# A two-layer transformer block on one Trainium2 core: latent attention's value product turned over, its probabilities divided first, and the order of work around the mixers changed

## The chip, the cores and the metric

The kernel runs on one core of a Trainium2 chip. The time is that of the device for one execution, in microseconds (us), median of several runs; lower is better. The engines are TensorE (PE in the rows; its weight loads are PEld), VectorE (DVE), ScalarE (ACT), GpSimd (POOL), and SyncE (SP), which issues most of the transfers.

## The reference

Two layers, each of three sublayers on 256 tokens of width 1024: a gated feed-forward (width 2816), a mixer, another feed-forward. Around each stands a modulation from the condition `c` and a layer norm of the scaled residual. The mixer of layer 0 is a hybrid of windowed attention and a gated recurrence; that of layer 1 is latent attention:

```python
def mla(h, pos, w_down, q_norm, kv_norm, w_uq, w_ukv, w_out):
    cq, ckv, kr = jnp.split(h @ w_down, [C_Q_RANK, C_Q_RANK + C_KV_RANK], axis=-1)
    q = (rms_norm(cq, q_norm) @ w_uq).reshape(bsz, seq, C_HEADS, C_NOPE + C_ROPE)
    kv = (rms_norm(ckv, kv_norm) @ w_ukv).reshape(bsz, seq, C_HEADS, C_NOPE + C_V)
    ...
        s = (jnp.einsum('bqhd,bkhd->bhqk', qn_i, k_nope)
             + jnp.einsum('bqhr,bkr->bhqk', qr_i, k_rope)).astype(F32) * scale
        p = jax.nn.softmax(s, axis=-1).astype(v.dtype)
        return jnp.einsum('bhqk,bkhd->bqhd', p, v)
    ...
    return o.swapaxes(0, 1).reshape(bsz, seq, C_HEADS * C_V) @ w_out
```

There are 16 heads with keys of 64+32 and values of 64. Everything is float32.

## The kernel before

Tokens lie in two tiles of 128 (t = 0, 1). A projection is three matmuls: each factor is split into a high part and the rest (`w_hi`/`w_lo` for weights, `hT_hi`/`hT_lo` for the transposed activations), and hi*hi, lo*hi and hi*lo are added in PSUM (`product`, L1910, L1913, L1914). Weights come in slots of up to 128x2048 through three raw buffers; ScalarE rounds a slot into `w_hi` (`split_hi`), VectorE subtracts to get `w_lo` (`split_lo`, L1231), and a matmul on a slot waits on `lo_ready` of it. The six sublayers run one after another: feed-forward, hybrid, feed-forward, feed-forward, latent attention (MLA), feed-forward. Between sublayers a seam normalizes the residual, transposes it on TensorE (`enter`, `enter_second`) and makes `hT_hi`/`hT_lo` on ScalarE and VectorE.

Latent attention works in 16 units m of two heads and one token tile (`mla_unit`), heads in four groups g of four. The order on every engine comes from a list written out by hand, `mla_plan`; VectorE has its own, `mla_vector_plan`. Round n holds S of unit n (scores, two 96-deep matmuls of 256 columns, L2032; VectorE takes the negated maximum, L1734; ScalarE takes the exponential and its sum, L1104), P of unit n-1 (four transposes of the probabilities, L2043; VectorE copies them out as `mpT`, L1740, and takes the reciprocal of the sum, L1744) and V of unit n-2 (values, four matmuls with the probabilities stationary, 64 columns each, L2055; ScalarE scales by the reciprocal into `m_o`, L1113). The tables `before` and `behind` put the pieces of the projections uq and ukv, the transposes of queries and keys (`qkT`, L2022), the splits of weights and the pieces `out` of the output projection around the rounds. `owin` transposes `m_o` (four times four transposes, L2068), ScalarE and VectorE take its high and low part (L1122, L1753), and `out` multiplies with it. V uses one PSUM bank, bank 5, so V of a unit waits until the unit before it is out of that bank: in this kernel on `o_att`, which ScalarE raises behind L1113.

The hybrid mixer has one list for all engines, `hybrid_plan`. In a feed-forward, `take_lo` (L1790) makes the low part of the gated activations, and ScalarE's first `silu` (L1007) needs another activation table than what a mixer leaves loaded.

Of the kernel before, what the change touches and what calls it, by code (L numbers as in the profile page):

```python
# [13 lines left out]
F32 = mybir.dt.float32  # L14
# [29 lines left out]
def build(nc, A, out):  # L44
# [11 lines left out]
    with ExitStack() as ctx:  # L56
# [34 lines left out]
        neg_half = sb("neg_half", [P, 1])  # L91

# [173 lines left out]
        rden_ready = sem("rden_ready")  # L266
        freq_ready = sem("freq_ready")
# [120 lines left out]
        def hybrid_plan():  # L388

            yield from (("proj", 0), ("proj", 1), ("enter", 1), ("split", 3), ("lb", 0), ("proj", 2),  # L390
                        ("piece", 56), ("piece", 57), ("split", 4), ("scale", 0), ("split", 5), ("lb", 1), ("proj", 3), ("split", 6), ("kT", 0),
# [24 lines left out]

        OWIN = (0, 3)
# [9 lines left out]
        def mla_plan():  # L427
# [6 lines left out]
            before = {1: (("rq", (1, 1)),), 3: (("qkT", (1, 0)),), 4: (("uq", (2, 0)), ("rq", (2, 0))),  # L434
                      5: (("uq", (2, 1)), ("rq", (2, 1))), 6: (("ukv", (2, 0)),), 7: (("qkT", (2, 0)), ("ukv", (2, 1))),
                      8: (("uq", (3, 0)), ("rq", (3, 0)), ("uq", (3, 1))), 9: (("rq", (3, 1)), ("ukv", (3, 0)), ("ukv", (3, 1))),
                      12: (("out", (0, 0, 0)),), 13: (("out", (0, 0, 1)),), 14: (("out", (1, 0, 0)),), 15: (("out", (1, 0, 1)),),
                      16: (("out", (2, 0, 0)),)}
            behind = {1: (("hi", (7, 0, 1)),), 2: (("hi", (8, 0, 1)),), 3: (("qkT", (1, 1)),), 4: (("hi", (9, 0, 1)),),
# [13 lines left out]
            yield from (("out", (3, 0)), ("split", (16, 0, 1)), ("owin", (1, 1)), ("end", 0), ("out", (0, 1)), ("out", (1, 1)),  # L453
                        ("out", (2, 1)), ("next", 0), ("out", (3, 1)))

        def mla_vector_plan():
# [5 lines left out]
            inner = {1: (("rq", (1, 1)),), 11: (("owin", (0, 0)),), 12: (("owin", (1, 0)),), 15: (("owin", (0, 1)),)}  # L462
# [6 lines left out]
            for n in range(18):  # L469
                if n < 16:  # L470
                    yield "S", n
                yield from inner.get(n, ())
                if n == 9:
                    yield "qkT", (3, 0)
                if 0 < n < 17:
                    yield "P", n - 1
# [1987 lines left out]
```

## Time and profile before

| | |
|---|---|
| median of 3 runs | 1029.35 us (1028.67 to 1029.74) |
| profiled execution | 1028.7 us, its span 1026.7 us |
| TensorE busy | 1000.4 us, 97% of the span |
| VectorE / ScalarE busy | 807.3 us (79%) / 501.8 us (49%) |
| MLA, 725 to 850 us from the span's start | TensorE 122.38 of 125 us busy, VectorE 102.66, ScalarE 81.89 |

A row of a timeline gives start, duration, engine, line, operation, operands and count; in brackets stands the engine's idle time before it and what ended that. The ends of matmuls are modelled and overlap their successors, so the pace of TensorE is read from starts, not from durations.

### The profile page before, as it was taken

The page shows a single profiled execution, that of the slowest core. Times are in us where ns is not written, and L with a number is a line of the kernel's source. Part 1 is how long each engine was busy: PE and PEld are TensorE (multiplying, and loading weights), DVE is VectorE, ACT ScalarE, POOL GpSimd, SP SyncE. Part 2 cuts the span into 40 slices and gives each one's busy share as a digit, 9 for nine tenths or more (in the row PEclk, how much of TensorE's full clock was granted, in tenths as well). Part 3 has the DMA queues.
Part 4 walks back from the last instruction along what each step waited for, and adds up shares of the span by engine and source line. Part 5 has one row for each costly group of instructions (what it writes and reads, how often), then busy time and mean ns, then how long its engine had stood idle before and what let it go on. Part 6 is the DMA issues. An engine that isn't in the chain of part 4 may idle for free.

```text
span 1026.7 us, 13208 instructions
## 1 busy us (share of the span) xinstructions
PE 1000.4 (97%) x5024; PEld 830.1 (81%) x5024; DVE 807.3 (79%) x1203; ACT 501.8 (49%) x754; POOL 47.6 (5%) x101
## 2 busy tenths in 40 slices
PE   7999999999999999999999999999999999999996
PEld 5678888879978788888887888888888878888885
DVE  5989898678989897888778878877788886666455
ACT  4654344366767544343545343443677554444430
POOL 1000000011311000000000000000100000000000
PEclk9999999999999999999999999999999999999999
DMA  9999998458423699979848997974323559656431
GB/s 352 409 363 409 385 373 317 161 185 278 154 108 120 207 379 343 318 276 340 296 149 317 337 325 274 386 252 136 93 98 101 165 180 332 230 203 242 168 123 41
DMA packets 72545, 254.80 MB, mean 248 GB/s; under 512 B 8801, under 2 KB 10337, under 8 KB 72482
## 3 DMA queue, kind: packets, MB, share of 16 engines
q1 hardware_dynamic: 68946, 242.91, 65.5%
q0 software_dynamic: 3104, 10.39, 3.1%
q8 instruction: 40, 0.66, 0.2%
q10 hardware_dynamic: 432, 0.66, 0.2%
q14 instruction: 23, 0.19, 0.1%
HBM read 252.85 MB, written 1.07 MB: 247 GB/s over the span
## 4 chain that ended last, share of the span: by engine, by line
PE 82%; DVE 7%; ACT 4%; DMA 4%; issue 2%; DVEq 0%; SPq 0%; ACTq 0%
PE bank L1910 25%; PE bank L1914 24%; PE bank L1913 24%; DMA w_raw<-in_w_dram 3%; PE bank L2321 2%; DVE w_lo L1231 2%; DMA arena<-in_ada_w_dram 1%; PE bank L2032 1%; PE bank L2055 1%; PE bank L2022 1%; ACT w_hi L885 1%; PE bank L2043 1%; ACT arena L919 1%; ACT hT_hi L913 0%; PE bank L1883 0%
## 5 line engine op out<-in xcount | busy, mean ns | idle before, releaser
L1231 DVE TENSOR_TENSOR w_lo<-w_raw,w_hi 128x2048 fp32r<-128x2048 f32 (+3 forms) x162 | 345.1, 2149 | 25.5 <-ACT w_hi L885 25.5
L1910 PE MATMUL bank<-w_hi,hT_hi 128*128 128x512 f32 (+3 forms) x880 | 351.2, 399 | 8.9 <-DVE hT_lo L1769 4.2
L1914 PE MATMUL bank<-w_lo,hT_hi 128*128 128x512 f32 (+3 forms) x880 | 338.9, 385 | 0.0
L1913 PE MATMUL bank<-w_hi,hT_lo 128*128 128x512 f32 (+3 forms) x880 | 338.3, 384 | 0.0
L885 ACT ACTIVATE w_hi<-w_raw 128x2048 fp32r<-128x2048 f32 (+3 forms) x152 | 281.1, 1852 | 37.3 <-DMA w_raw<-in_w_dram 27.1
L1910 PEld LDWEIGHTS bank<-w_hi,hT_hi 128*128 128x128 f32 x880 | 165.9, 189 | 44.9 <-DVE hT_lo L1769 5.9
L1914 PEld LDWEIGHTS bank<-w_lo,hT_hi 128*128 128x128 f32 x880 | 165.7, 188 | 33.5
L1913 PEld LDWEIGHTS bank<-w_hi,hT_lo 128*128 128x128 f32 x880 | 166.4, 189 | 28.7
L1007 ACT ACTIVATE arena<-bank 128x256 f32<-128x256 f32 x88 | 33.6, 382 | 279.8 <-PE bank L1914 279.7
L1250 DVE SCALAR_TENSOR_TENSOR arena<-arena,c_row 128x1024 f32<-128x1024 f32 x131 | 155.8, 1219 | 8.0 <-ACT c_row L960 7.7
L1910 PE MATMUL bank<-w_hi,fT_hi 128*128 128x512 f32 x352 | 138.4, 393 | 1.1 <-DVE fT_lo L1790 0.7
L1914 PE MATMUL bank<-w_lo,fT_hi 128*128 128x512 f32 x352 | 137.4, 390 | 0.0
L1913 PE MATMUL bank<-w_hi,fT_lo 128*128 128x512 f32 x352 | 137.1, 389 | 0.0
L1785 DVE TENSOR_TENSOR arena<-arena,bank 128x256 f32<-128x256 f32 x88 | 36.9, 419 | 77.7 <-ACT arena L1007 77.6
L1790 DVE TENSOR_TENSOR fT_lo<-bank,fT_hi 128x256 fp32r<-128x256 f32 x88 | 37.2, 423 | 57.6 <-ACT fT_hi L1011 57.6
L1910 PEld LDWEIGHTS bank<-w_hi,fT_hi 128*128 128x128 f32 x352 | 66.1, 188 | 16.2 <-issue 1.7
L1914 PEld LDWEIGHTS bank<-w_lo,fT_hi 128*128 128x128 f32 x352 | 66.1, 188 | 13.9
L1913 PEld LDWEIGHTS bank<-w_hi,fT_lo 128*128 128x128 f32 x352 | 66.1, 188 | 13.2
L1011 ACT ACTIVATE fT_hi<-bank 128x256 fp32r<-128x256 f32 x88 | 33.7, 383 | 78.3 <-PE bank L2321 78.3
L1910 PE MATMUL bank<-hT_hi,w_hi 128*128 128x256 f32 x128 | 36.6, 286 | 0.5 <-DVE w_lo L1231 0.5
L1914 PE MATMUL bank<-hT_lo,w_hi 128*128 128x256 f32 x128 | 36.2, 283 | 0.0
L1913 PE MATMUL bank<-hT_hi,w_lo 128*128 128x256 f32 x128 | 36.2, 283 | 0.0
(242 smaller groups left out, 863.3 us busy)
## 6 DMA issues: line engine op xcount, KB each, us to landing
w_raw<-in_w_dram SPq DMA_DIRECT2D x306, 512.0 KB, 5.6
arena<-in_ada_w_dram SPq DMA_DIRECT2D x132, 512.0 KB, 7.3
m_o<-in_ada_w_dram SPq DMA_DIRECT2D x10, 512.0 KB, 6.9
gate_row<-gate_scratch POOLq DMA_DIRECT2D x6, 512.0 KB, 5.0
arena<-in_ln_g_dram POOLq DMA_DIRECT2D x6, 512.0 KB, 4.8
arena<-in_ln_b_dram POOLq DMA_DIRECT2D x6, 512.0 KB, 6.1
w_raw<-in_w_dram SPq DMA_DIRECT2D x8, 256.0 KB, 2.8
w_raw<-in_w_dram SPq DMA_DIRECT2D x8, 192.0 KB, 2.8
```

What stands on the lines that cost most here:

```text
L885: nc.scalar.activation(w_hi[:, j0 % RING, 0:n], raw_of(j0)[:, 0:n], ACT.Copy).then_inc(hi_ready, 1)
L919: op = nc.scalar.activation(scratch[:, k * P:(k + 1) * P], second_block(s, k), ACT.Identity, bias=mod_B[:, s, k:k + 1], scale=mod_G[:, s, ...
L1007: nc.scalar.activation(sg[:, i % 2, :], unit_bank(s, i)[:, 0:CW], ACT.Silu).then_inc(silu_done, 1)
L1011: nc.scalar.activation(fT_hi[:, i % 2, :], T[i % 2][:, 0:CW], ACT.Copy).then_inc(fT_hi_ready, 1)
L1231: op = nc.vector.tensor_tensor(w_lo[:, j0 % RING, c], raw_of(j0)[:, c], w_hi[:, j0 % RING, c].bitcast(F32), ALU.subtract)
L1250: nc.vector.scalar_tensor_tensor(out=raw, in0=raw, scalar=1.0, in1=c_row[:, :], op0=ALU.mult, op1=ALU.mult, accum_out=mod_col[:, a:a + 1]) ...
L1785: nc.vector.tensor_tensor(hid[:, i % 2, :], sg[:, i % 2, :], unit_bank(s, i)[:, CW:2 * CW], ALU.mult)\
L1790: nc.vector.tensor_tensor(fT_lo[:, i % 2, :], T[i % 2][:, 0:CW], fT_hi[:, i % 2, :].bitcast(F32), ALU.subtract).then_inc(fT_ready, 1)
L1910: mm = nc.tensor.matmul(dst, a_hi, b_hi, start=start, stop=False)
L1913: nc.tensor.matmul(dst, a_lo, b_hi, start=False, stop=False)
L1914: return nc.tensor.matmul(dst, a_hi, b_lo, start=False, stop=stop)
L2321: mm = nc.tensor.transpose(T[i % 2][:, q * P:(q + 1) * P], hid[:, i % 2, q * P:(q + 1) * P], ident[:, :])
```

## The change

In MLA: V's operands change places, so that the values (128x64 of a head) are stationary and the transposed probabilities move (128 columns); the two heads of a unit write partitions 0 to 63 and 64 to 127 of bank 5, and the output is transposed already. ScalarE copies it to `hT_hi` (new stage V there) and VectorE subtracts for `hT_lo` (`values_lo`, L1766 of the new kernel); V of a unit now waits on `o_ready`, which VectorE raises behind that subtraction. `m_o`, the `owin` stages and their evictions go. The probabilities are divided before they are transposed: stage D on VectorE takes the reciprocal and multiplies the two heads' probabilities in place, and P waits on `p_ready`. The copy of the transposed probabilities moves from VectorE to ScalarE. The latent activations move to k = 4 to 7 of `hT_hi`/`hT_lo`. The output bank of token tile 1 is 6 and 7, so that `out` pieces of it can stand inside the rounds, and the tables are written anew.

Elsewhere: ScalarE runs a one-element Silu before the entry of the feed-forward behind a mixer; VectorE splits slot 2 of a feed-forward before `take_lo` of its first unit; in the hybrid, ScalarE enters the second token tile before it evicts projection 1, and splits and pieces change places.

```diff
+        def mla_block(m):
+            g, t, p = mla_unit(m)
+            return 2 * g + p, slice(t * P, (t + 1) * P)
+        M_UNITS = {(0, 0): 2, (0, 1): 4, (1, 0): 6, (1, 1): 8, (2, 0): 10, (3, 0): 12, (2, 1): 14, (3, 1): 16}
...
+            before = {4: (("uq", (2, 0)),), 5: (("uq", (2, 1)),), 6: (("ukv", (2, 0)),), 3: (("qkT", (1, 0)),),
+                      7: (("qkT", (2, 0)), ("ukv", (2, 1))), 8: (("uq", (3, 0)), ("uq", (3, 1))),
+                      9: (("ukv", (3, 0)), ("ukv", (3, 1))), 10: (("out", (0, 0)),), 11: (("out", (0, 1)),),
+                      12: (("out", (1, 0, 0)),), 13: (("out", (1, 0, 1)),), 14: (("out", (2, 0)),), 15: (("out", (3, 0)),),
+                      16: (("out", (1, 1)),), 17: (("out", (2, 1)),)}
...
+            for n in range(16):
+                yield from early.get(n, ())
+                yield "S", n
+                if n >= 3:
+                    yield "V", n - 3
                 yield from inner.get(n, ())
+                yield "D", n
                 yield from outer.get(n, ())
-            yield from (("split", (16, 0, 1)), ("owin", (1, 1)), ("end", 0))
+            yield from (("end", 0), ("V", 15), ("lo", (16, 1)), ("scale", (1, 1)))
...
# ScalarE
+                        elif stage == "P":
+                            act.wait_ge(p_tr, A0 + m + 1)
...
+                            nc.scalar.activation(mpT[:, m % 2, :], banks[4][:, :], ACT.Copy).then_inc(pT_ready, 1)
                         elif stage == "V":
+                            k, tok = mla_block(m)
                             act.wait_ge(pv_done, A0 + m + 1)
...
+                            nc.scalar.activation(hT_hi[:, k, tok], banks[5][:, 0:P], ACT.Copy).then_inc(o_hi, 1)
...
+                    if early_third(s - 1):
+                        nc.scalar.activation(early_silu[:, :], neg_half[:, :], ACT.Silu)
...
# VectorE
-                        norm(s, 0)
+                        values_lo(13)
+                        norm(s, 0, lambda: (values_lo(14), split_lo(base[s] + 16, (0,))))
...
-                        nc.vector.tensor_copy(mpT[:, m % 2, :], banks[4][:, :]).then_inc(pT_ready, 1)
+                    elif stage == "D":
+                        b = m % 2
                         dve.wait_ge(s_exp, A0 + m + 1)
...
+                        step(nc.vector.reciprocal(rden[:, m % 4, :], den[:, m % 4, :]))
+                        step.wait()
+                        for a in range(2):
+                            op = nc.vector.tensor_scalar(mP[:, b, a, :], mP[:, b, a, :], rden[:, m % 4, a:a + 1], None, ALU.mult)
+                        op.then_inc(p_ready, 1)
...
+            def values_lo(m):
+                k, tok = mla_block(m)
+                dve.wait_ge(o_hi, O0 + m + 1)
+                nc.vector.tensor_tensor(hT_lo[:, k, tok], banks[5][:, 0:P], hT_hi[:, k, tok].bitcast(F32),
+                                        ALU.subtract).then_inc(o_ready, 1)
...
+                        if i == 0:
+                            split_lo(base[s] + 2)
                         take_lo(i)
...
# TensorE
-                        pe.wait_ge(s_exp, A0 + m + 1)
+                        pe.wait_ge(p_ready, m + 1)
...
-                            pe.wait_ge(o_att, A0 + m)
-                        for a in range(2):
-                            h = 2 * p + a
-                            for kt in range(NT):
-                                c = (2 * a + kt) * P
-                                mm = nc.tensor.matmul(banks[5][:, a * 64:a * 64 + 64], mpT[:, m % 2, c:c + P],
-                                                      v_nat[g][:, kt, h * 64:h * 64 + 64],
-                                                      start=kt == 0, stop=kt == 1)
+                            pe.wait_ge(o_ready, O0 + m)
+                        for kt in range(NT):
+                            for a in range(2):
+                                h, c = 2 * p + a, (2 * a + kt) * P
+                                mm = nc.tensor.matmul(banks[5][a * 64:a * 64 + 64, 0:P], v_nat[g][:, kt, h * 64:h * 64 + 64],
+                                                      mpT[:, m % 2, c:c + P], start=kt == 0, stop=kt == 1,
+                                                      skip_group_check=True)
                         mm.then_inc(pv_done, 1)
-                    elif stage == "owin":
...
-                        for k in range(4):
-                            c = (4 * half + k) * P
-                            mm = nc.tensor.transpose(banks[6 + t][:, k * P:(k + 1) * P], m_o[:, t, c:c + P], ident[:, :])
```

VectorE's queue in rounds 12 and 13 of MLA, before; each row is an instruction and the semaphores it waits on (`COPY` is the eviction of the transposed probabilities, `w_lo` the split of half a slot, `x<-x,arena` the scaling by the norm's rows):

```order
L1734 TENSOR_REDUCE neg_max<-bank2 128x2 [waits s_exp,s_done]
L1753 TENSOR_TENSOR hT_lo<-bank7,hT_hi 128x4x128 [waits o_hi]
L1740 COPY spare_row<-bank4 128x512 [waits pv_done,p_tr]
L1744 RECIPROCAL rden<-den 128x2 [waits o_att,s_exp]
L1231 TENSOR_TENSOR w_lo<-w_raw,w_hi 128x1024 [waits hi_ready]
L1672 TENSOR_TENSOR x<-x,arena 128x1024 [waits dve_step]
L1734 TENSOR_REDUCE neg_max<-bank3 128x2 [waits s_exp,s_done]
L1740 COPY spare_row<-bank4 128x512 [waits pv_done,p_tr]
L1744 RECIPROCAL rden<-den 128x2 [waits o_att,s_exp]
L1231 TENSOR_TENSOR w_lo<-w_raw,w_hi 128x1024 [waits hi_ready]
```

VectorE's queue in round 14 and up to D of round 15, after (`hT_lo<-bank5` is `values_lo`; the first `w_lo` of the `x2` row is the second half of the slot of `out` (3, 0)):

```order
L1749 TENSOR_REDUCE neg_max<-bank2 128x2 [waits s_exp,s_done]
L1766 TENSOR_TENSOR hT_lo<-bank5,hT_hi 128x128 [waits o_hi]
L1244 TENSOR_TENSOR w_lo<-w_raw,w_hi 128x1024 [waits hi_ready]
L1754 RECIPROCAL rden<-den 128x2 [waits s_exp]
L1757 TENSOR_SCALAR arena<-arena,rden 128x256 [waits dve_step]
L1757 TENSOR_SCALAR arena<-arena,rden 128x256
L1244 TENSOR_TENSOR w_lo<-w_raw,w_hi 128x1024 [waits hi_ready] x2
L1749 TENSOR_REDUCE neg_max<-bank3 128x2 [waits s_exp,s_done]
L1766 TENSOR_TENSOR hT_lo<-bank5,hT_hi 128x128 [waits o_hi]
L1244 TENSOR_TENSOR w_lo<-w_raw,w_hi 128x1024 [waits hi_ready]
```

The subtraction that frees bank 5 stands behind the maximum of the same round, and the multiplications of D stand between the two halves of a slot.

TensorE's queue in round 14 and at the beginning of round 15, after (bank 2 and 3 hold scores, bank 4 the transposed probabilities, bank 5 the values' product; `lo_ready4` is the slot of `out` (3, 0)):

```order
L2053 MATMUL bank2<-arena 128x256 [waits s_exp,qk4_ready]
L2053 MATMUL bank2<-arena 128x256
L2064 MATMUL bank4<-ident,arena 128x128 [waits pT_ready,p_ready]
L2064 MATMUL bank4<-ident,arena 128x128 x3
L2075 MATMUL bank5<-spare_row,arena 64x128 [waits o_ready,pT_ready]
L2075 MATMUL bank5<-spare_row,arena 64x128 x3
L1930 MATMUL bank0<-w_hi,hT_hi 128x512 [waits lo_ready4,o_ready]
```

In the kernel before, the row of V reads as this, in the same place between P and the next piece:

```order
L2043 MATMUL bank4<-ident,arena 128x128 [waits pT_ready,s_exp]
L2043 MATMUL bank4<-ident,arena 128x128 x3
L2055 MATMUL bank5<-arena,spare_row 128x64 [waits o_att,pT_ready]
L2055 MATMUL bank5<-arena,spare_row 128x64 x3
```

V's wait changed from ScalarE's semaphore to VectorE's, P's from the exponential to the division, and an output piece stands where a projection stood.

## Rows read from the trace of the kernel before

**Rows 1.** The page: busy time, and the chain that ended last by engine

```profile
PE 1000.4 (97%) x5024; PEld 830.1 (81%) x5024; DVE 807.3 (79%) x1203; ACT 501.8 (49%) x754; POOL 47.6 (5%) x101
PE 82%; DVE 7%; ACT 4%; DMA 4%; issue 2%; DVEq 0%; SPq 0%; ACTq 0%
```

**Rows 2.** Busy time by stage: PE, PEld, DVE, ACT, POOL, PEclk, DMA share, GB/s

```profile
725.00:850.00 125.00, 122.38 (x738) 106.08 (x738) 102.66 (x202) 81.89 (x210) 5.13 (x8) 1.00 0.40 134
```

**Rows 3.** Timeline of one round of MLA: start, us, engine, instruction

```profile
774.04 1.03 PE L2032 MATMUL bank<-arena 96*128 96x256 f32 x4
...
774.91 0.60 PE L2043 MATMUL bank<-ident,arena 128*128 128x128 f32 x4
775.11 0.69 DVE L1734 TENSOR_REDUCE neg_max<-bank 128x2 f32<-128x512 f32 x1 [0.73 <-PE bank L2032]
775.35 1.00 PE L2055 MATMUL bank<-arena,spare_row 128*128 128x64 f32 x8
775.72 0.68 DVE L1740 COPY spare_row<-bank 128x512 f32<-128x512 f32 x1
775.83 0.47 ACT L1104 ACTIVATE arena<-bank,neg_max 128x256 f32<-128x256 f32 x1 [0.75 <-DVE neg_max L1734]
776.19 1.04 PE L2022 MATMUL bank<-ident,arena 128*96 128x128 f32 x8
...
776.75 0.51 ACT L1113 ACTIVATE m_o<-bank,rden 128x64 f32<-128x64 f32 x2
```

**Rows 4.** Chain of waits, in the hybrid: scores of two heads

```profile
307.51 0.63 PE bank L2185 x4
```

**Rows 5.** Groups by line and shape: count, busy us, mean ns, idle before

```profile
L1278 DVE TENSOR_TENSOR hT_lo<-arena,hT_hi 128x128 fp32r<-128x128 f32 x10 | 2.5, 288 | 1.9 <-ACT hT_hi L913 1.5
...
L1744 DVE RECIPROCAL rden<-den 128x2 f32<-128x2 f32 x16 | 2.5, 155 | 0.0
...
L1562 DVE TENSOR_SCALAR arena<-arena 128x64 f32<-128x64 f32 x16 | 3.6, 270 | 0.0
...
L1469 DVE TENSOR_SCALAR x<-x,mean_var,rstd 128x1024 f32<-128x1024 f32 x5 | 4.1, 814 | 3.4 <-POOL rstd L779 3.4
...
L1231 DVE TENSOR_TENSOR w_lo<-w_raw,w_hi 128x1024 fp32r<-128x1024 f32 x14 | 16.9, 1210 | 1.3 <-ACT w_hi L885 1.3
...
L1395 DVE TENSOR_TENSOR arena<-bank,gate_row 128x512 f32<-128x512 f32 x12 | 7.7, 685 | 4.3 <-PE bank L1914 4.3
...
L1192 ACT ACTIVATE win_pT<-bank 128x512 f32<-128x512 f32 x8 | 4.7, 588 | 0.0
```

**Rows 6.** Timeline of TensorE: first P, and scores of unit 4

```profile
755.03 0.66 PE L2043 MATMUL bank<-ident,arena 128*128 128x128 f32 x4
...
762.80 1.03 PE L2032 MATMUL bank<-arena 96*128 96x256 f32 x4
```

**Rows 7.** Timeline of TensorE: half an output piece, a wait, the next entry

```profile
809.53 0.50 PE L1910 MATMUL bank<-w_hi,hT_hi 128*128 128x512 f32 x1
...
811.05 0.60 PE L2043 MATMUL bank<-ident,arena 128*128 128x128 f32 x4
...
789.32 1.13 PE L2032 MATMUL bank<-arena 96*128 96x256 f32 x4 [0.78 <-DVE arena L1725]
...
826.07 1.03 PE L1883 MATMUL bank<-ident,x 128*128 128x128 f32 x8
```

**Rows 8.** Timeline around the seams: a table load, and TensorE's waits

```profile
837.12 1.28 ACT L1007 ACT_TABLE_LOAD   x1
...
840.46 0.50 PE L1910 MATMUL bank<-w_hi,hT_hi 128*128 128x512 f32 x1 [0.69 <-DVE hT_lo L1285]
...
358.30 0.50 PE L1910 MATMUL bank<-w_hi,hT_hi 128*128 128x512 f32 x1 [0.71 <-DVE hT_lo L1285]
...
549.65 0.47 PE L1910 MATMUL bank<-w_hi,fT_hi 128*128 128x512 f32 x1 [0.47 <-DVE w_lo L1231]
...
218.87 0.63 PE L1896 MATMUL bank<-ident,x 128*128 128x128 f32 x4 [1.08 <-issue]
```

More of the change, by code:

```diff
@@ L388, in hybrid_plan @@
         def hybrid_plan():
-            yield from (("proj", 0), ("proj", 1), ("enter", 1), ("split", 3), ("lb", 0), ("proj", 2),
-                        ("piece", 56), ("piece", 57), ("split", 4), ("scale", 0), ("split", 5), ("lb", 1), ("proj", 3), ("split", 6), ("kT", 0),
+            yield from (("proj", 0), ("proj", 1), ("enter", 1), ("lb_pre", 0), ("split", 3), ("split", 4), ("lb", 0), ("proj", 2), ("hi", 5),
+                        ("piece", 56), ("lo", 5), ("piece", 57), ("scale", 0), ("lb", 1), ("proj", 3), ("split", 6), ("scale", 1), ("kT", 0),
                         ("proj", 4), ("split", 7), ("proj", 5), ("piece", 58), ("split", 8), ("proj", 6),
@@ L415, in hybrid_plan, with hybrid_scalar_plan @@
                         ("out", (3, 1)))
+        def hybrid_scalar_plan():
+            yield from (("proj", 0), ("enter", 0), ("enter", 1), ("proj", 1))
+            plan = hybrid_plan()
+            for stage, m in plan:
+                if (stage, m) == ("enter", 1):
+                    break
+            yield from plan
         OWIN = (0, 3)
@@ L452, in mla_plan @@
                 yield from behind.get(n, ())
-            yield from (("out", (3, 0)), ("split", (16, 0, 1)), ("owin", (1, 1)), ("end", 0), ("out", (0, 1)), ("out", (1, 1)),
-                        ("out", (2, 1)), ("next", 0), ("out", (3, 1)))
+            yield from (("next", 0), ("out", (3, 1)))
         def mla_vector_plan():
@@ L548, in out_banks @@
         def out_banks(s, t):
-            return ([banks[0], banks[5]], [banks[6], banks[7]])[t] if subs[s][0] == "hyb" else Y[t]
+            if subs[s][0] == "ffn":
+                return Y[t]
+            return ([banks[0], banks[5 if subs[s][0] == "hyb" else 1]], [banks[6], banks[7]])[t]
         def entry_banks(s):
@@ L718, in _ @@
                         if kind == "hyb":
[L719 removed]
+                            for a in {7: (58,), 8: (59,), 12: (60,), 13: (61,), 14: (62, 63)}.get(j - base[s], ()):
                                 ada_piece(a)
@@ L1496, in hybrid @@
                     elif stage == "scale":
-                        scale_shift(s, 0)
-                        scale_shift(s, 1)
+                        scale_shift(s, m)
                     elif stage in ("split", "lo"):
                         split_lo(base[s] + m)
-                    elif stage == "lb" and m == 0:
+                    elif stage == "lb_pre":
                         logits = cols[:, 96:108].rearrange("p (v h) -> p v h", v=3)
@@ L1509, in hybrid @@
                         op.then_inc(lb_pre, 1)
-                    elif stage == "lb":
+                    elif stage == "lb" and m == 1:
                         dve.wait_ge(lb_exp, 1)
@@ L1832, in _ @@
                             split_lo(base[s] + n)
-                        if i == 0 and not early_third(s):
-                            split_lo(base[s] + 2)
                         for n in end_slots(i):
@@ L1999, in mla @@
                             w, tok = slice(k * width, (k + 1) * width), slice(t * P, (t + 1) * P)
-                            mm = product(bank[:, 0:width], hT_hi[:, 2 * v + k, tok], hT_lo[:, 2 * v + k, tok],
+                            at = M_LATENT + 2 * v + k
+                            mm = product(bank[:, 0:width], hT_hi[:, at, tok], hT_lo[:, at, tok],
                                          w_hi[:, j0 % RING, w], w_lo[:, j0 % RING, w], k == 0, k == 1)
@@ L2078, in hybrid @@
+                        out_project(s, i, t, MOUT, range(4), {i: O0 + M_UNITS[i, t]}, q or (0, 1))
             def hybrid(s):
```

87 lines of the change are left out of this document (26 added, 61 removed), and 13 rows, old and new, of tables (behind, inner, outer).

## The prediction

> **What bounds the kernel now.** I read the page first: TensorE is busy 97% of the span and holds 82% of the chain that ended last, VectorE 7%, ScalarE and the transfers 4% each [rows 1]. So time goes when TensorE's stream gets shorter, and comes when TensorE waits. Then the table of stages: from 725 to 850 us, around latent attention (MLA), TensorE is busy 122.38 of 125 us at a granted clock of 1.00 (the 2.4 GHz level), VectorE 102.66 [rows 2]. Its waits there are few; the largest in the rounds is 0.78 us [rows 7]. Then one round in time [rows 3]: S starts at 774.04, P at 774.91, V at 775.35, the next work at 776.19. TensorE's pace is thus 0.87 for S, 0.44 for P, 0.84 for V, with nothing between. VectorE begins the maximum 0.20 behind the start of P, and its next instruction comes 0.61 later. I call the end of S (start of P) T in what follows.
>
> **The change part by part, TensorE's own work.** V has 4 matmuls, recorded as 8 passes, 0.105 us each, though they move only 64 columns. After, they move 128. A pass of 256 columns takes 0.87/4 = 0.217 [rows 3], so one of 128 takes 0.108. If the two heads' column halves work side by side, a pass of one head lies over a pass of the other. No instruction of the trace uses column halves. The nearest is the hybrid's scores, two heads in row halves, four passes of 256 columns: 0.63 us, three passes' time, not four [rows 4]. By that pattern 8 passes take the time of 5: 0.54 us, 0.30 less than before. The other bound is no overlap, 8 x 0.108 = 0.86, 0.02 more. I take the pattern of rows 4: 16 x 0.30 = -4.8. The four groups of transposes of `m_o` go, each like a P: 4 x 0.44 = -1.8. The 0.78 wait before a score [rows 7] goes with the copy that left VectorE's queue. TensorE in MLA: -7.4.
>
> Against the pattern stands a rule of the Trainium skill (TensorE: Matmul & The Clock Gate, Part 3, The mechanism): a weight load overlaps a matmul in flight only when the two are in different row groups. Column halves share their rows. By that rule each pass would show its load as well; if a load of 64 columns takes half of V's present pace, 0.053, V would take 8 x (0.108 + 0.053) = 1.29 us, 0.45 more than before, and the sum would be 12.0 higher, 1050. The trace does not bear it out: V's passes follow each other at 0.105 us with full-height loads between them [rows 3], so such loads are already hidden. I give it 2%.
>
> **What V waits for.** This decides the result. V of a unit needs bank 5 free of the unit before. Before, ScalarE freed it a round earlier. Now VectorE does, and its queue has, in round n, the maximum of unit n, then `values_lo` of unit n-3; TensorE has, in round n, S of n, P of n-1, V of n-2, which needs exactly that `values_lo`. So V cannot start before T + 0.20 + 0.61 (maximum, rows 3) + 0.29 (a 128x128 subtraction, rows 5) + about 0.05 for the semaphore = T + 1.15. P ends at T + 0.44. TensorE stands for 0.71 us; queued behind V are the projections, the output pieces and the next S, on which VectorE and ScalarE wait in turn. Rounds 4 to 8 and 10 to 15 have it: 11 x 0.71 = +7.8. In round 9 a transpose stage lies between and covers it, but the second one then waits about 0.5 for its bank: +0.5.
>
> D: reciprocal 0.16 [rows 5], a step's wait, two multiplications of 256. Rows 5 give 0.27 for 64 columns and 0.81 for 1024 as bounds; by the line between them 256 take about 0.38, the second overlapping a little. D takes some 0.9. The exponentials end near T + 1.95 (776.75 plus the last readout, rows 3), so P of the next round is free at T + 2.9 to 3.2. From round 3 on, T' is at least 3.7 later, so D costs TensorE nothing there.
>
> At the start it does. VectorE now waits for the first exponential (ready by 755.03, where P starts, rows 6) and divides before it takes the second maximum. P of unit 0 starts 1.0 later. The second exponential starts near 756.6, and behind it ScalarE has the eviction of a ukv piece and the new copy of the probabilities (0.59, rows 5): P of unit 1 finds its bank copied only at about 759.1, with TensorE idle for 1.9. Then V of unit 1 waits for `values_lo` behind a half split, D and a pair of copies: about 1.6. Unit 4's scores start near 766.7 instead of 762.80 [rows 6]. That is +3.9 with two V savings inside, +4.5 of waits.
>
> **Output pieces.** A half split takes 1.21 [rows 5]. `out` (1, 0) and (2, 0) stand right behind V, at T + 1.69, but their slot's second half is split behind `values_lo`, done at T + 2.3: 0.65 each, +1.3. `out` (3, 0) is worse: its second half stands behind D, ends near T + 4.4, and TensorE is there at T + 1.69: +2.7.
>
> **The end of MLA.** An output piece takes two times 1.52 less overlap, about 2.8 [rows 7]. With T the end of the last S: P, V of 13, `out` (1, 1), P of 15 end at T + 5.0; V of 14 needs `values_lo(13)`, which now stands behind D (T + 3.1) and the four 512-wide instructions of the residual (0.6 to 0.69 each, rows 5), T + 5.9: +0.9. The next entry's transposes (826.07 in the kernel before, rows 7) come without a wait. But behind them VectorE has `values_lo(15)`, a half split and a scaling of 1.2 each before it enters the feed-forward, which puts TensorE's first product there 0.8 late, and the second tile's entry about 1.2 more. Tail: +2.9.
>
> MLA in sum: -7.4 + 7.8 + 0.5 + 4.5 + 1.3 + 2.7 + 2.9 = +12.3.
>
> **Seams and hybrid.** The early Silu takes the 1.28 table load [rows 8] out of the path to the second entry; ScalarE was idle before it. That ends the waits of 0.69 and 0.71 [rows 8]. The third split before `take_lo` ends one of 0.47 [rows 8]. In the hybrid, ScalarE stood behind projection 1 while TensorE waited 1.08 for the entry [rows 8]; now it enters first. Half of this can return at the weight splits that come next. I take 1.0. Sum: -2.9. ScalarE has room for the copies it takes on (49% busy, rows 1).
>
> Total +9.4 on the profiled 1028.7, or on the median 1029.35: 1038.7. Estimates of small waits tend to add what overlaps, so I round down to 1038.
>
> The Trainium skill (TensorEngine Tiling (Array Packing), Key Properties) says that a change of tiling mode drains TensorE, and V would change it twice a unit, 32 times. It gives no figure; rows 4 show three full passes in 0.63 us between full-height work, so nothing of a drain is visible for row halves. At the 0.16 us between a 1.03 us modelled duration and the 0.87 pace [rows 3], 32 would make +5.1, and the sum 1043.
>
> **The rivals.**
> 1. No overlap of the halves, or a drain at each switch (12%): then V costs 0.02 more, not 0.30 less; +5.1, 1043. For it: no row has column halves. Against it: rows 4. Nothing hides it, since V is on the path in every round.
> 2. Faster (19%): V's wait doesn't bind. This holds if `values_lo` is done when P ends, that is when VectorE needs under T + 0.44 for what stands before it; it decides from there, since each tenth more costs 1.1 us over 11 rounds. Then -7.4 - 2.9 = -10.3 remain, less waits at the start that are there anyway: about 1019 to 1023. Against it: the maximum cannot start before S ends and takes 0.61 alone.
> 3. It cancels (6%): V's wait is real (+8.3), but the weight splits, the start and the end cost about 2 instead of 11.4, since the engines behind catch up: near 1029.
> 4. The gain is not made at all in V because VectorE becomes the bound: its round is then 0.61 + 0.29 + 1.21 + 0.9 + 1.2 = 4.2, against 4.1 on TensorE in round 11. That is a part of the forecast's upper end, not a case of its own.
>
> **How the numbers follow.** Forecast 61%, 1033 to 1042 around 1038; rival 1 12%, rival 2 19%, rival 3 6%, loads in the open 2%. What a measurement can tell from no change is 0.2%, 2.1 us. Slower than 1031.4: 0.75; within: 0.05; faster than 1027.3: 0.20. The range of 8 in 10 takes in rivals 1 and 3 and the edge of 2: 1026 to 1044.
>
> **What would show it.** In the profile after: V's row 64x128 at 0.54 us pace (0.86 shows rival 1); in nearly each round a wait of TensorE of about 0.7 before V, released by VectorE's `hT_lo` (none shows rival 2); a wait of about 2.7 on `w_lo` before the first matmul of `out` (3, 0); P of unit 1 some 2.5 us later than before against S of unit 0; no table load between the entries; the waits at the three seams gone. The prediction is wrong if VectorE's `values_lo` is done before P ends, or if the rounds close up elsewhere.

## The result, and the profile after

The changed kernel takes 1039.53 us (median of 4 runs, 1038.78 to 1040.37) against 1029.01 of the kernel before beside it: ratio 1.0102, 95% interval [1.0084, 1.0119]. The profiled span grew from 1026.7 to 1037.0 us. In the page, against [rows 1]:

```profile
PE 997.6 (96%) x5008; PEld 823.2 (79%) x5008; DVE 807.7 (78%) x1233; ACT 504.4 (49%) x752; POOL 51.3 (5%) x101
PE 84%; DVE 7%; DMA 4%; ACT 3%; issue 2%; SPq 0%; DVEq 0%; ACTq 0%
```

TensorE is busy for 2.8 us less and stands idle for 13 us more. The table of stages shows where (columns as [rows 2]):

```profile
725.00:750.00 25.00, 24.35 (x156) 21.62 (x156) 18.46 (x53) 17.06 (x48) 2.69 (x4) 1.00 0.36 111
750.00:775.00 25.00, 19.70 (x137) 15.74 (x137) 19.37 (x53) 18.31 (x51) 0.00 (x0) 1.00 0.29 97
775.00:800.00 25.00, 21.42 (x136) 17.48 (x135) 16.55 (x40) 14.32 (x37) 0.00 (x0) 1.00 0.27 93
800.00:825.00 25.00, 19.18 (x104) 14.87 (x104) 16.19 (x29) 13.51 (x31) 0.00 (x0) 0.93 0.35 114
825.00:850.00 25.00, 22.99 (x123) 17.36 (x123) 20.70 (x44) 12.69 (x30) 2.45 (x4) 1.00 0.38 121
sum 125.00, PE 107.64 PEld 87.08 DVE 91.26 ACT 75.88 POOL 5.14; mean PE 21.53 PEld 17.42 DVE 18.25 ACT 15.18 POOL 1.03
```

Where 122.38 of 125 us were busy, 107.64 are, though no engine is full: VectorE fell from 102.66 to 91.26. In one stage the granted clock is 0.93, not 1.00. TensorE's waits over the whole kernel, by what ended them (total, times, longest):

```profile
PE bank L2075 <- DVE hT_lo L1766: 8.4, 13, 1.0
...
PE bank L1930 <- DVE w_lo L1244: 3.3, 3, 2.3
...
PE bank L1930 <- DVE fT_lo L1810: 2.3, 2, 1.9
...
PE bank L2064 <- ACT spare_row L1134: 1.4, 1, 1.4
PE bank L2053 <- DVE arena L1740: 1.2, 1, 1.2
PE bank L2064 <- DVE arena L1757: 1.0, 1, 1.0
```

L2075 is V, waiting for `values_lo`; L1930 with `w_lo` is an output piece waiting for the split of its slot; L2064 is P at the start. The wait on `fT_lo` is in the feed-forward layers, not in latent attention. One round of the new kernel in time, to be read beside [rows 3]:

```profile
771.06 1.03 PE L2053 MATMUL bank<-arena 96*128 96x256 f32 x4
...
771.92 0.60 PE L2064 MATMUL bank<-ident,arena 128*128 128x128 f32 x4
772.12 0.69 DVE L1749 TENSOR_REDUCE neg_max<-bank 128x2 f32<-128x512 f32 x1 [0.74 <-PE bank L2053]
772.73 0.28 DVE L1766 TENSOR_TENSOR hT_lo<-bank,hT_hi 128x128 fp32r<-128x128 f32 x1
...
773.16 0.66 PE L2075 MATMUL bank<-spare_row,arena 128*64 128x128 f32 x8 [0.63 <-DVE hT_lo L1766]
...
773.75 1.08 PE L2043 MATMUL bank<-ident,arena 128*96 128x128 f32 x8
```

S starts at 771.06, P 0.86 later, the maximum 0.20 behind P, `values_lo` 0.61 behind the maximum, and V 1.24 behind P, with 0.63 idle. V's pace is 773.75 - 773.16 = 0.59, where it was 0.84 (0.81 in front of a projection). The idle times are counted from modelled ends; by starts a V that need not wait stands 0.53 behind P (best2 below), so the wait moved it by 0.70. The fourth output piece shows the largest wait, and something that was not forecast:

```profile
818.80 0.31 PE L2075 MATMUL bank<-spare_row,arena 128*64 128x128 f32 x2
821.44 0.51 PE L1930 MATMUL bank<-w_hi,hT_hi 128*128 128x512 f32 x1 [2.33 <-DVE w_lo L1244]
821.75 0.63 PE L1933 MATMUL bank<-w_hi,hT_lo 128*128 128x512 f32 x1
822.18 0.63 PE L1934 MATMUL bank<-w_lo,hT_hi 128*128 128x512 f32 x1
822.60 0.63 PE L1930 MATMUL bank<-w_hi,hT_hi 128*128 128x512 f32 x1
```

and the stages there; the granted clock is the third number from the end of each row:

```profile
821.00:822.00 1.00, 0.56 (x2) 0.55 (x3) 1.00 (x2) 1.00 (x1) 0.00 (x0) 0.86 0.00 0
822.00:824.00 2.00, 2.00 (x6) 1.51 (x6) 0.43 (x1) 0.56 (x1) 0.00 (x0) 0.50 0.76 174
824.00:825.00 1.00, 1.00 (x4) 0.81 (x3) 0.00 (x0) 0.00 (x0) 0.00 (x0) 0.50 0.98 385
```

TensorE had worked 0.66 us in the 3.6 before 821.44. Then the granted clock fell from 1.00 to 0.50 (2.4 to 1.2 GHz), matmuls came every 0.43 us instead of 0.23, and the piece took 821.44 to 825.85, 4.41 us, where the third took 2.83.

### The profile page after: what moved, and what is told of

Its sections match the earlier page's. It is cut to its first block, busy times and chain, and to the rows that moved or that the text cites. A ratio compares the mean times of both kernels' runs of the same rounds, so it can differ in the third digit from the quotient of the medians.

```text
span 1037.0 us, 13173 instructions
## 1 busy us (share of the span) xinstructions
PE 997.6 (96%) x5008; PEld 823.2 (79%) x5008; DVE 807.7 (78%) x1233; ACT 504.4 (49%) x752; POOL 51.3 (5%) x101
## 4 chain that ended last, share of the span: by engine, by line
PE 84%; DVE 7%; DMA 4%; ACT 3%; issue 2%; SPq 0%; DVEq 0%; ACTq 0%
PE bank L1930 26%; PE bank L1934 26%; PE bank L1933 26%; DMA w_raw<-in_w_dram 3%; PE bank L2330 2%; DMA arena<-in_ada_w_dram 1%; DVE w_lo L1244 1%; PE bank L2053 1%; DVE neg_max L1749 1%; PE bank L2152 1%; PE bank L2075 1%; PE bank L2182 0%; PE bank L2043 0%; DVE x L1431 0%; ACT arena L939 0%
## 5 line engine op out<-in xcount | busy, mean ns | idle before, releaser
L1930 PE MATMUL bank<-w_hi,hT_hi 128*128 128x512 f32 (+3 forms) x880 | 351.5, 399 | 12.0 <-DVE hT_lo L1789 4.9
L1930 PEld LDWEIGHTS bank<-w_hi,hT_hi 128*128 128x128 f32 x880 | 166.4, 189 | 49.6 <-DVE hT_lo L1789 6.2
L1930 PE MATMUL bank<-w_hi,fT_hi 128*128 128x512 f32 x352 | 138.2, 393 | 2.3 <-DVE fT_lo L1810 2.3
L1930 PEld LDWEIGHTS bank<-w_hi,fT_hi 128*128 128x128 f32 x352 | 66.1, 188 | 16.2 <-DVE fT_lo L1810 2.9
L1930 PE MATMUL bank<-hT_hi,w_hi 128*128 128x256 f32 x128 | 36.5, 285 | 0.0
```

Of the source, the lines that this page charges most:

```text
L1930: mm = nc.tensor.matmul(dst, a_hi, b_hi, start=start, stop=False)
```

## The experiments

Milestones on TensorE make the traces comparable: when S of unit 0 starts, how long it is from there to the first transpose of the next layer's entry (latent attention), and from there to the start of the last matmul. All times in us:

| kernel | median | S of unit 0 | latent attention | after it |
|---|---|---|---|---|
| before | 1028.7 | 751.60 | 74.47 | 191.7 |
| changed | 1039.5 | 748.74 | 87.83 | 191.5 |
| seams_hybrid | 1023.6 | 748.06 | 74.47 | 190.1 |
| hybrid_alone | 1026.3 | 748.98 | 74.45 | 192.5 |
| seams_alone | 1026.1 | 751.77 | 74.46 | 190.1 |
| latent_alone | 1043.3 | 751.93 | 87.83 | 192.8 |
| heads_in_turn | 1038.8 | 748.00 | 87.80 | 191.6 |
| vlo_first | 1033.5 | 747.78 | 82.96 | 191.5 |
| slot14_early | 1036.2 | 748.79 | 84.35 | 191.5 |
| two_maxima | 1037.4 | 747.41 | 86.66 | 191.5 |
| best1 | 1026.1 | 748.35 | 76.08 | 191.0 |
| best2 | 1023.1 | 747.80 | 73.27 | 191.0 |
| best2b | 1025.4 | 748.06 | 75.28 | 190.9 |
| best3 | 1023.8 | 748.35 | 74.28 | 190.2 |

The median of the kernel before is the one beside the experiments (1028.53 to 1028.74 there). The third column varies by 1.4 among kernels that have the same instructions up to there as the changed one (747.41 to 748.79), so the fourth is the one that tells edits in latent attention apart.

**vlo_first.** Is V's wait a matter of VectorE's order?

```diff
-                yield "S", n
                 if n >= 3:
                     yield "V", n - 3
+                yield "S", n
```

> The changed kernel with one line of VectorE's order moved: in each round of latent attention values_lo of the unit three back stands ahead of the maximum, not behind it. TensorE's instructions are unchanged. Theory (V waits for values_lo only because it is queued behind the maximum): the 13 waits of 0.63 us in front of V (8.4 us by the waits view) go, or nearly, and what comes instead is at most the maximum 0.28 us later, which the exponential and then P may pass on in a few rounds: 1032 us against 1039.5 now (1030 to 1034). Rival 1 (VectorE or the chain of maximum, exponential, division is the bound of the round, so the wait only moves): the waits turn up in front of P or S with the same sum, 1038 to 1040. Rival 2 (the four V matmuls in alternate column halves cost the time, not the wait): no change, 1039.5.

1033.51 us, 6.0 less than the changed kernel, of which 4.9 lie in latent attention (the other 1.0 ahead of it, where the instructions are the same). TensorE's waits there:

```profile
PE bank L1930 <- DVE w_lo L1244: 4.8, 3, 2.9
...
PE bank L2053 <- DVE arena L1740: 2.2, 2, 1.9
...
PE bank L2075 <- DVE hT_lo L1766: 1.3, 2, 0.9
```

V's wait went from 8.4 to 1.3. Some of it came back (slots +1.5, a key and query copy +1.0), since TensorE now reaches the splits sooner. The theory holds; rivals 1 and 2 do not.

**slot14_early.** Did the clock fall because of the wait?

In short form (`inner` stands between maximum and division of a unit, `outer` behind the division):

```diff
-  inner 14: (("lo", (14, 0)),)     outer 13: (("scale", (1, 0)),)   outer 14: (("lo", (14, 1)),)
+  inner 14: (("lo", (14, 1)),)     outer 13: (("lo", (14, 0)),)     outer 14: (("scale", (1, 0)),)
```

> The changed kernel with the two halves of the split of weight slot 14 one step earlier on VectorE (in units 13 and 14), the scaling of x behind them. Theory: the wait of 2.33 us in front of the fourth output piece (821.44) goes, and with it the fall of TensorE's granted clock behind it, which made that piece 4.4 us long where the second and third piece took 2.8: 1039.5 - 2.3 - 1.6 = 1035.6 us. Rival 1 (the clock falls for what TensorE did before, not for the wait): the wait goes and the fall stays, 1037.2. Rival 2 (VectorE is the bound there, and the wait only moves to the third piece or the last V): 1039 to 1040.

1036.16 us, -3.4; latent attention 3.48 shorter. In the profiled execution (1035.39 us) the wait is 0.48 and the clock stays:

```profile
818.00:821.00 3.00, 2.04 (x14) 1.64 (x15) 2.96 (x7) 2.82 (x8) 0.00 (x0) 1.00 0.13 33
821.00:824.00 3.00, 2.93 (x16) 2.23 (x14) 1.94 (x3) 1.60 (x1) 0.00 (x0) 1.00 0.91 307
```

2.33 - 0.48 = 1.85 of wait and 4.41 - 2.83 = 1.58 of clock make the 3.4 between the two profiled executions. In vlo_first, whose slot wait is 2.89, the clock fell at the same place (0.50 from 817 to 820); in best3, whose longest wait in latent attention is 1.92, it did not. But this is one execution of each kernel. The fall in the changed kernel's trace lasted 3.4 us, which lowers the mean clock of an execution by about 0.0016, and the mean clock of the other executions of slot14_early is 0.997, 0.995, 0.996 and 0.996, against 0.998 in the profiled one (0.997 or 0.998 in every execution of best1, best2 and best3). The three at 0.995 and 0.996 are also its slowest, 1036.2 to 1037.4 us. So the clock very likely fell in them too, at a place that no trace shows: the edit took the fall away in the execution that was profiled, not in all.

**heads_in_turn.** Do the column halves run beside each other because the matmuls alternate between them?

```diff
-                        for kt in range(NT):
-                            for a in range(2):
+                        for a in range(2):
+                            for kt in range(NT):
```

> The changed kernel with V's four matmuls in another order: both of head a=0 (columns 0 to 63), then both of a=1, where now they alternate between the halves. Theory (the change's 0.59 us from start to next start, against 0.84 before, comes from alternating halves that run beside each other): V takes 0.75 to 0.85 us, 16 units at +0.16 to +0.26 are +2.5 to +4 us, less what the wait for values_lo takes back where V's end sets nothing: 1041.5 to 1043.5. Rival (four passes in 64 columns cost what they cost, and the order of halves is nothing): 1039.5.

1038.82 us; latent attention 87.80 against 87.83. V in the trace:

```profile
764.39 0.67 PE L2075 MATMUL bank<-spare_row,arena 128*64 128x128 f32 x8 [0.63 <-DVE hT_lo L1766]
764.99 0.45 PE L1930 MATMUL bank<-w_hi,hT_hi 128*128 128x384 f32 x1
```

Pace 0.60, as before the edit. My theory falls: the order of halves is nothing here. That they do overlap is shown all the same, since eight passes of 128 columns one behind another would take 0.86. The records of a V in either kernel have the starts of passes in pairs: 0.00, 0.01, 0.13, 0.17, 0.24, 0.28, 0.35, 0.39 us (changed kernel, V at 778.15), the next instruction at 0.59. Two by two at 0.109 a pair, and 0.20 from the last pass to the next work. How the hardware pairs them when the program issues one half first is open.

**seams_hybrid, hybrid_alone, seams_alone.** What do the side edits give? The first is the kernel before with both, the others with one each (in short form):

```diff
 (hybrid)  order of ScalarE: ("proj", 0), ("enter", 0), ("enter", 1), ("proj", 1); splits and pieces as in the change
 (seams)   + nc.scalar.activation(early_silu[:, :], neg_half[:, :], ACT.Silu)   ahead of the entry behind a mixer
 (seams)   + if i == 0: split_lo(base[s] + 2)   ahead of take_lo(0)
```

> The kernel before with only the side edits of the change: the hybrid layer's new order and the edits at the seams; latent attention is as before. Prediction on record for this part: -2.9 us, so 1026.1. By the trace of the changed kernel, first product of latent attention against before: -2.85 us, so 1026.2, if nothing is given back later. Rival (latent attention's start gives it back, since its weights then come too late or its first entry waits): 1028 to 1029.5, and then the latent part of the change costs only 10.5 us instead of 13.4.

> The kernel before with only the hybrid layer's new order, no seam edits. By the offsets between the traces, the hybrid layer gave 2.4 us up to its end (my price was 1.0): 1028.7 - 2.4 = 1026.3 us. Rival (the hybrid order only brings TensorE earlier to transfers and the seam gives it back, and the seam edits are what makes it stay): 1028 or more.

> The kernel before with only the seam edits of the feed-forward layers (the table of SiLU loaded early, the split of weight slot 2 ahead of take_lo). Both parts together measured -5.1 us. If the parts add up: -5.1 + 2.4 = -2.7, so 1026.0 us. My price on record was 0.69 + 0.71 + 0.47 = -1.9, so 1026.8. Rival (the table load is hidden without the hybrid order as well as with it, nothing gained): 1028.7.

1023.57 us together (ratio 0.9955 [0.9941, 0.9968]), 1026.32 and 1026.06 alone: -5.2, -2.2 and -2.5 against the before beside each. The hybrid's part shows by S of unit 0 (751.60 to 748.98): the wait of 1.08 [rows 8] is gone, and so are two that were in no sum, 0.53 for a split at 231.33 and 0.48 at 282.37 (0.07 is left of it). The seams' part shows only in the last layer (191.7 to 190.1), where the wait of 0.69 [rows 8] is gone (0.96 is gained at that place, the rest over the layer; that column varies by 0.8 between before and hybrid_alone, which have the same instructions there). Behind the hybrid the waits of 0.71 and 0.47 [rows 8] are gone too, but in seams_alone one of 1.05 for `fT_lo` stands in their place (at 371.11), and S of unit 0 comes at 751.77, no earlier than before. Expectation for the sum was 1026.1: missed by 2.5.

**latent_alone.** The change without the side edits.

> The change without its side edits: latent attention new, the hybrid layer's order and the seams as before. If the two halves of the change add up: the side edits gave -5.1 on the kernel before, the whole change is +10.5, so latent attention alone is +15.6: 1028.6 + 15.6 = 1044.2 us. By the traces' offsets (side edits gave only 2.85 us by the start of latent attention, and the last feed-forward layer in the changed kernel keeps 0.9 us of waits for its second entry, which the side edits alone do not have): 1028.6 + 13.4 = 1042 us. Rival on record (latent attention without overlap of the column halves costs more, and hides behind the seams' gain): 1046 or more.

1043.32 us, ratio 1.0148 [1.0134, 1.0162]: +14.6, between the two sums. So the side edits give 3.8 in the changed kernel and 5.2 in the kernel before, by the medians; by the traces' milestones it is 4.5 and 5.1 (3.2 and 1.3 against 3.5 and 1.6), so most of the difference is within what the traces vary. One source of that is seen: after the hybrid's seam TensorE waits for `take_lo`, which waits for ScalarE, which waits for a transfer of weights (6.03 us in the changed kernel). Depending on when the transfer landed, TensorE's wait was 1.86 us in the changed kernel (at 368.15), 1.0 in heads_in_turn and 0.5 in vlo_first, with the same instructions.

**two_maxima.** The start of latent attention: maximum 1 ahead of division 0.

```diff
                 yield "S", n
+                if n == 0:
+                    continue
+                if n == 1:
+                    yield "D", 0
```

> The changed kernel with one edit at latent attention's start on VectorE: the maximum of unit 1 stands ahead of the division of unit 0, not behind it. Theory (at the start P of unit 1 waits 1.44 us for ScalarE's copy, which stands behind the exponential of unit 1, which waits 1.5 us for its maximum, which is queued behind the division that waits for unit 0's exponential): the exponential of unit 1 starts 1.4 us earlier and P of unit 1 with it, 1039.5 - 1.4 = 1038.1 us. Rival (TensorE's next instructions wait for the division of unit 1 and for values_lo anyway, so the wait moves by a few rows): 1039.5.

1037.44 us (-2.1); latent attention 1.17 shorter. P of unit 1 no longer waits:

```profile
751.69 0.65 PE L2068 MATMUL bank<-ident,arena 128*128 128x128 f32 x4 [1.00 <-DVE arena L1761]
753.21 0.66 PE L2068 MATMUL bank<-ident,arena 128*128 128x128 f32 x4
```

Of the 1.44, 0.25 came back in V of unit 1 (a wait of 1.21 there, 0.96 in the changed kernel). The theory holds; the rest of the 2.1 lies ahead of the edit, inside the variation of the third column.

**best1, best2, best2b, best3.** Is the loss VectorE's order alone? TensorE's instructions are those of the change in all four.

```diff
 best1:  + "V", n-3 ahead of "S", n;  "S", 1 ahead of "D", 0;  qkT (2,1) ahead of lo (11,0);  scalings of x behind the splits
         + outer 10: lo (12,1)   outer 11: lo (13,0)   inner 12: lo (13,1)   inner 13: lo (14,0)   outer 13: lo (14,1)
         + values_lo(13) ahead of residual(s)
 best2b: + "V", n-2 behind "D", n instead;  inner 12: lo (13,0)   outer 12: lo (13,1)
 best2:  + best2b, and ScalarE's hi (14,1) behind unit 12
 best3:  + best2, qkT (1,0), (1,1) ahead of lo 7, lo 8;  the scalings of x one place earlier each
```

> The changed kernel with VectorE's order in latent attention made for the new waits: values_lo of three units back ahead of the maximum; maximum 1 ahead of division 0; the key and query copies (2,1) ahead of the split of slot 11; the halves of the splits of slots 12, 13 and 14 one step earlier and the scalings of x behind them; values_lo(13) ahead of the residual. TensorE's instructions are unchanged. Theory (waits on VectorE's order are the whole loss, the four V matmuls themselves are cheaper than before): 1039.5 - 6.0 (values_lo first, measured) - 3.4 (slot 14, measured) - 1.4 (start) - 1.9 (copies (2,1)) - 1.4 (slots 12 to 14, 0.48 each) - 0.9 (values_lo(13)) = 1024.5 us, so 1024 to 1028, about the kernel before with the side edits alone (1023.6). Rival (VectorE and the chain maximum, exponential, division fill the round, so waits come back in other places): 1030 or more.

> As best1, with values_lo two units back directly behind the division instead of three units back ahead of the maximum; the halves of the split of slot 13 behind maximum and division of unit 12; and on ScalarE the second half of the split of slot 14 one unit earlier. Theory (the waits left in best1's latent attention, 0.62 + 1.07 + 0.77 in front of V and 0.57 in front of P, come from VectorE instructions queued in front that wait for ScalarE's split, not from VectorE's amount of work): 1026.1 - 3.0 = 1023.1 us, so 1022.5 to 1024.5, level with or ahead of the kernel before with the side edits alone (1023.6). Rival (VectorE is full there and the waits come back elsewhere): 1025.5 to 1027.

> best2 without ScalarE's edit: the split of slot 14's second half stays behind unit 13. Theory: both halves of VectorE's split of slot 14 wait for ScalarE's second half, so the division of unit 13, which is queued behind the first, is late by about 1.5 us, of which 0.6 to 1.4 reaches TensorE: 1023.7 to 1024.5, about 1 us above best2. Rival (the slack in front of P of unit 13, a whole output piece, hides it): as best2.

> best2 with the last waits that its trace shows in latent attention taken up, on VectorE alone: the key and query copies (1,0) and (1,1) ahead of the splits of slots 7 and 8 (S of unit 4 waits 1.10 us for a copy behind such a split), and the four scalings of x one place earlier each, so that none stands between the last unit and the entry of the next layer (the second entry's first product waits 0.67 us). Theory: 1023.1 - 1.1 - 0.7 = 1021.3 us, 1020.8 to 1022.5, ahead of the kernel before with the side edits alone (1023.6). Rival (S of unit 4 is early by nothing, since the weights' split that was put behind is late for the up-projection instead, and the entry waits for ScalarE): 1022.5 to 1023.5.

1026.12, 1023.10, 1025.39 and 1023.83 us. best2 has latent attention in 73.27 us, 1.2 less than the kernel before, and its stages are nearly full again (19.70, 21.42 and 19.18 in the changed kernel):

```profile
750.00:775.00 25.00, 22.87 (x162) 18.22 (x161) 20.68 (x56) 19.82 (x58) 0.00 (x0) 1.00 0.38 125
775.00:800.00 25.00, 24.18 (x152) 19.57 (x151) 19.36 (x44) 15.00 (x39) 0.00 (x0) 1.00 0.30 108
800.00:825.00 25.00, 24.47 (x144) 19.21 (x144) 24.21 (x46) 15.05 (x38) 0.56 (x1) 1.00 0.43 142
```

TensorE waits five times up to the next entry, twice for under 0.5. The three longest waits are these, and behind them stand those of best2b, which show what ScalarE's order was worth:

```profile
752.07 0.66 PE L2068 MATMUL bank<-ident,arena 128*128 128x128 f32 x4 [1.00 <-DVE arena L1761]
760.97 1.13 PE L2057 MATMUL bank<-arena 96*128 96x256 f32 x4 [1.10 <-DVE arena L1744]
...
821.07 1.09 PE L1907 MATMUL bank<-ident,x 128*128 128x128 f32 x8 [0.53 <-DVE x L1487]
```

```profile
808.24 0.66 PE L2068 MATMUL bank<-ident,arena 128*128 128x128 f32 x4 [0.92 <-DVE arena L1761]
809.66 0.47 PE L1934 MATMUL bank<-w_hi,hT_hi 128*128 128x512 f32 x1 [0.18 <-DVE w_lo L1248]
...
823.34 1.09 PE L1907 MATMUL bank<-ident,x 128*128 128x128 f32 x8 [1.12 <-DVE x L1487]
```

0.92 + 0.18 and 0.59 more at the entry are 1.7 of the 2.0 between them in latent attention (2.3 by the medians). The theory had this price too low (0.6 to 1.4), and the rival, which gave it none, is out. best1 stands 1.6 above its theory's number, by waits that best2 then took up. best3 missed its range (1020.8 to 1022.5), and its rival's too (up to 1023.5): the wait of 1.10 became 1.92.

```profile
762.39 1.13 PE L2057 MATMUL bank<-arena 96*128 96x256 f32 x4 [1.92 <-DVE arena L1744]
```

VectorE in unit 2 of best3 tells why:

```profile
754.19 0.69 DVE L1753 TENSOR_REDUCE neg_max<-bank 128x2 f32<-128x512 f32 x1
755.97 0.17 DVE L1758 RECIPROCAL rden<-den 128x2 f32<-128x2 f32 x1 [1.09 <-ACT arena L1131]
...
758.10 0.94 DVE L1248 TENSOR_TENSOR w_lo<-w_raw,w_hi 128x768 fp32r<-128x768 f32 x1
758.96 0.68 DVE L1753 TENSOR_REDUCE neg_max<-bank 128x2 f32<-128x512 f32 x1
```

Between a maximum and its division VectorE waits 1.09 us for the exponential anyway. In best2 the split of slot 7 fills that hole at no cost; moved behind, it delays the next maximum: 10.61 us behind S of unit 0 here, 9.74 in best2 (757.54), and the whole chain with it. The scalings' part worked (the last column, 191.0 to 190.2).

best2 against seams_hybrid is 0.9948 [0.9934, 0.9961] against 0.9955 [0.9941, 0.9968] of the same before: not told apart by the medians. best2 is faster than both the kernel before and the changed one. The turned product with the best order found is thus 1.2 us shorter inside latent attention than the old one and 0.9 longer behind it (191.0 against 190.1): no gain over the side edits alone is shown.

Why only 1.2, when V itself is cheaper by 0.25 in each of 16 units? P pays part of it, and waits of 1.00 and 1.10 us that the kernel before does not have take the rest. A round of best2, in which V waits for nothing, and the column halves that the kernel before already has, in stage A of the hybrid (L2143):

```profile
772.85 0.60 PE L2068 MATMUL bank<-ident,arena 128*128 128x128 f32 x4
773.38 0.66 PE L2079 MATMUL bank<-spare_row,arena 128*64 128x128 f32 x8
773.97 1.08 PE L2047 MATMUL bank<-ident,arena 128*96 128x128 f32 x8
```

```profile
264.54 0.61 PE L2143 MATMUL bank<-arena 128*128 128x128 f32 x4
265.08 0.67 PE L2143 MATMUL bank<-arena,spare_row 128*64 128x64 f32 x10
```

From P to V it is 0.53 by starts, where it was 0.44 [rows 3]. The records of the passes show where: the first pass of V starts 0.20 us behind the last pass of P, in 15 of best2's 16 units, and 0.11 in 15 of the 16 before. P and V together take 0.53 + 0.59 = 1.12 against 0.44 + 0.84 = 1.28 (1.25 in front of a projection). That is 0.13 to 0.16 a unit, 2.1 to 2.6 us in all. Whether the 0.09 in front of V is a drain of the array was not tested apart.

## Why the prediction was right

The forecast was 1038.0, the measured 1039.5, and the main cause is the one forecast: V waits for a `values_lo` that stands behind the maximum. vlo_first takes that cause away alone and gets 4.9 us of latent attention back, 6.0 by the medians. The closeness of the total owes something to errors that cancel, so here are the terms:

- *V's own time.* Forecast 0.54, measured 0.59. But P, in front of it, takes 0.53 by starts where 0.44 was counted, so the two together fell by 0.13 to 0.16 a unit: about -2.3, not -4.8.
- *The row that was missed.* The prediction says that no instruction of the trace uses column halves. That is wrong: L2143 does, in the hybrid, with 64 columns stationary and outputs in partitions 0 to 63 and 64 to 127. Its passes of two halves start 0.01 apart (265.08), so that they run side by side, and the first starts 0.20 behind the last full-height one, not 0.11. The reading of [rows 4] was wrong in the same way: there, too, the first pass starts 0.20 behind the one before it, and two pairs of passes take 0.32 and 0.31, so something is lost at each side. That the pattern "8 passes take the time of 5" gave nearly the measured 0.59 was luck in part: the records show four pairs at 0.11 and 0.15 more at the borders.
- *Rival 1.* No overlap (0.86) is out. The loss at each switch is not: of the 0.32 a unit that the rival adds to the forecast, 0.14 is there (0.05 in V, 0.09 in front of it), 2.3 us of its 5.1. The Trainium skill's rule that a weight load overlaps only a matmul in another row group (TensorE: Matmul & The Clock Gate, Part 3, The mechanism) does not hold here. Column halves share their rows, and by that rule V would have taken 1.29; it took 0.59.
- *V's wait.* Forecast V at T + 1.15, 0.71 late, 11 times; measured T + 1.24, which is 0.70 behind the T + 0.53 of a V that does not wait. Right, by 0.01 a round.
- *Round 9.* Forecast 0.5, measured 0.45.
- *The start.* V of unit 1 waited 0.96, not 1.6. S of unit 4 came 14.28 us after S of unit 0, before 11.20: +3.1, forecast +3.9. P of unit 0 waited the forecast 1.0; P of unit 1 1.44, not 1.9.
- *Output pieces.* Forecast 0.65 twice and 2.7, measured 0.47 twice and 2.33. Missing in the sum was the clock, +1.6 in the profiled execution.
- *The end.* Forecast +0.9 for V of unit 14, measured 0.41; 0.8 for the first product of the feed-forward, measured 0.17; the second entry 1.2, measured 0.77. Too high throughout.
- *The wait before a score.* The 0.78 [rows 7] was counted as gone. S of unit 8 waits 1.16 in its place: 1.2 us missing in the sum.
- *Latent attention in sum.* Forecast +12.3, of which 2.0 lie behind the next entry's transposes. Up to there the forecast is +10.3 and the table has +13.4. With what lies behind, latent_alone has +14.6.
- *Side edits.* Forecast -2.9, measured -5.2 on the kernel before and -3.8 inside the change. The hybrid's order alone gave 2.2, priced at 1.0: half of the 1.08 was supposed to return at the splits and did not, and two waits of 0.5 that no sum had went too. The seams gave about what was forecast (1.6 by the table, 2.5 by the medians, against 1.9), but all of it in the last layer.

Latent attention was under-priced by 2.3 us, and the side edits by 0.9 inside the change; the sum, +9.4, came out 1.1 below the measured +10.5. Inside latent attention, too, terms that were too low (V and P, the score's wait, the clock) stand against others that were too high (the start, the output pieces, the end).

The edge that rival 2 named ("decides if `values_lo` is done by T + 0.44") turned out to be the right question asked too narrowly. In this order it is not reached, but the order is free: with VectorE's queue put in another order and one split of ScalarE's moved, the same TensorE instructions take 73.27 us instead of 87.83. Rival 3, that the engines catch up behind V's wait, did not happen.

## What to carry to other kernels

When a buffer's release moves to another engine, read what stands in front of the releasing instruction on that engine; here 0.61 us of a maximum, 13 times, cost more than the cheaper matmuls gave. Put filler (splits, scalings) into the places where the engine waits for a round trip anyway, here between a maximum and its division, and the release directly behind. Measure side edits apart: here they hid 3.8 us, a quarter, of a 14.6 us loss. And before saying that a trace has no example of an instruction's form, search it by form: the half-width matmuls of L2143 would have shown both the overlap and its price.

## What the hardware showed that was not expected

- TensorE's granted clock fell to 0.50 (1.2 GHz) behind waits of 2.33 and 2.89 us in which it had done little before, and the work behind took 1.6 us more. Five traces have such a wait in latent attention, and each has the fall. The traces whose longest wait there is 1.92 or less have none. No threshold follows from this: in three executions of slot14_early that were not profiled the clock very likely fell too (mean 0.995 and 0.996), and its longest wait in the profiled one is 1.44.
- Two heads in column halves: four pairs of passes at 0.109 us, 0.59 for the whole, independent of the order in which the halves are issued.
- Work in halves costs time at both sides: 0.20 us from the last full-height pass to V's first and 0.20 from V's last pass to the next work, where full-height passes stand 0.11 apart. In the kernel before, the column halves of L2143 and the row halves of L2185 start 0.20 behind the pass before them as well (eight of eight times and six of eight). This was read from records of passes, not tested by an experiment of its own.
